# A hybrid decoder step: last down part by column halves, squares beside it, its adds and the eighth mixed row on VectorE

## The chip, the cores and the metric

The kernel runs on one core of a Trainium2 chip. The metric is the device time of one execution in microseconds (us), the median of several runs. PE is TensorE (PEld its weight loads), DVE is VectorE, ACT is ScalarE, POOL is GpSimd, SP is SyncE, which issues most DMAs.

## What is computed

One layer over a prompt of 2048 tokens and eight samples of 4 tokens (2080 columns of 1024 channels): an mLSTM branch and a windowed attention branch, merged by sigmoid gates, and then a gated feed-forward block with a causal convolution, all in float32.

```python
ga, gb = jnp.split(jax.nn.sigmoid(gt), 2, axis=-1)
mixed = ga * (h_m @ p['w_a'][l]) + gb * (h_a @ p['w_b'][l])
x = x + mixed @ p['w_out'][l]
xn = rmsnorm(x, p['g_ffn'][l])
u = xn @ w_up                                   # 1024 -> 2 * 2816
c = b_conv + sum(w_conv[tap] * ext[:, tap:tap + S] for tap in range(3))
a, g = jnp.split(c, 2, axis=-1)
h = gelu(a) * g
x = x + h @ w_down                              # 2816 -> 1024
x = rmsnorm(x, p['g_final'])                    # mean of squares over the 1024 channels of a token
```

## The kernel before

Channels lie on the partitions (KT = 8 rows of 128), tokens on the columns. Every float32 product is made of a high and a low half of each operand: the weight's high half is written by ACT (`w_high`, L2469), its low half by DVE (`w_low`, L2719), and `product` issues two matmuls of high weights (L2376) for one of low weights (L2381) in each step of the sum.

Three phases follow each other; the change is in the last, `ffn_phase`. There every engine walks one list, `PLAN`, and does at each unit what belongs to it.

- **Spans.** Five spans of 416 columns. Each has eight `branch` units (row i of the mixed gates: DVE multiplies both gates by PSUM, L2888 and L2892; POOL adds the two, L2951; ACT and DVE split the sum into halves, L2503 and L2759) and eight `out` units (w_out). The norm of a span (column sum on PE, `root` on ACT, `invert` on DVE at L2764, `x_normed` at L2770) is taken during the next span; that of span 4, the last, during the first tiles of pair 0.
- **Column pairs.** Then three pairs of column halves (348, 348 and 344 columns each). A pair has 22 tiles of seven up products (`q` units, q2.6 being product 6 of tile 2), with Strassen sums of the input made by DVE and ACT (`prep_sums` L2781 to L2786, `prep_lows` L2792 to L2797, `prep_sums_high` L2521). DVE takes the products out of PSUM (`c22` L2805, `c21` L2811), applies the convolution (`taps`) and multiplies with the gelu (`product` L2831, `g_low` L2837).
- **Down parts.** Between the tiles stand six down parts of a pair, over 4, 4, 4, 4, 4 and 2 tiles. A `down` unit is one output row: two column halves into two of the three banks ps5, ps6 and ps7, which go round. Early parts are added into the residual by DVE (L2920). In pairs 0 and 1 the last two parts (`SEEDED` and above) are seeded: ACT writes the residual into PSUM ahead (L2582) and reads the sum back (L2587). In the last pair no part is seeded. The last part's product has six matmuls for a half.
- **Final norm.** `final_square` (ACT, L2620) squares a half row into a two-buffer ring, `final_total` (POOL, L2989) adds it up, `final_sum` (PE, L2396) sums over the partitions, `final_root` (ACT, L2626), `final_invert` (DVE, L2843), and `y_normed` (DVE, L2850) multiplies. For pairs 0 and 1 this lies in the next pair's first tiles; for the last pair it stands behind the last part, where `weighted` (ACT, L2631) has multiplied by the gain and DVE by the reciprocal (L2940).
- **Weights.** SP loads each unit's split weights into a ring of six chunks, `f_wh` and `f_wl` (L2224); in pair 0 they are made from float32 weights and stored (L2215).

## Time and profile before

| | us |
|---|---|
| three runs | 2860.35, 2861.37, 2864.24 |
| median | 2861.37 |
| the profiled execution's own time | 2858.3 |
| its span in the trace | 2856.5 |

The span is what the engines' records cover; 1.8 us lie around it. The profiled execution is 3.1 us below the median. In the trace `PE` is busy for 2764.0 us. The ffn phase runs from about 1100 us to the end: the five spans to 1424 us, pair 0 to 1894 us, pair 1 to 2368 us, pair 2 to 2835 us, and then the last norm.

A row of the timeline gives a start, a busy time, the engine, the line, what is written from what, and in square brackets how long the engine had been idle and whose instruction ended that.

### The profile page before, as it was taken

Reading aid. Unit: us, or ns where it says so; the run is one execution under the profiler, and the core shown is the slowest. Engines: PE = TensorE matmul, PEld = TensorE weight load, DVE = VectorE, ACT = ScalarE, POOL = GpSimd, SP = SyncE. Lnnn points to the kernel's source line nnn. Section 1 sums busy time; section 2 is a strip of 40 time slices with the busy share of each in tenths; the row PEclk is TensorE's granted clock in tenths of the full one; section 3 lists DMA queues with packets and bytes.
Section 4 is the critical chain, followed back from the end, with each engine's and each line's share of the span. In section 5 each row is a group of like instructions: output and inputs, shape, how many; then the busy total and the mean of one; then the engine's idle time right before and its main releaser. Section 6 shows DMA issues by size and latency. Waiting matters only on the chain. (4 is left out here: it accounts for less than half of the span.)

```text
span 2856.5 us, 47085 instructions
## 1 busy us (share of the span) xinstructions
PE 2764.0 (97%) x17306; PEld 2646.6 (93%) x17306; DVE 1747.3 (61%) x2752; ACT 1323.3 (46%) x2520; POOL 431.2 (15%) x663
## 2 busy tenths in 40 slices
PE   8999999999999999999989999999999999999997
PEld 8888799989998989999989999999999998999997
DVE  5212167676767668877887777856544456445554
ACT  4212235454555445555655444773443366333442
POOL 2111021211112222222200000020000003001112
PEclk9999999999999999999999999999999999999998
DMA  5534266556655458777676666767665566755654
GB/s 186 195 128 144 89 206 189 187 161 217 215 165 162 134 201 254 258 265 259 219 281 208 211 212 221 252 204 250 203 200 172 188 204 198 244 185 188 205 194 120
DMA packets 373684, 569.44 MB, mean 199 GB/s; under 512 B 50578, under 2 KB 197586, under 8 KB 373458
## 3 DMA queue, kind: packets, MB, share of 16 engines
q1 hardware_dynamic: 371346, 566.31, 60.3%
q8 instruction: 141, 2.31, 0.3%
q14 instruction: 85, 0.70, 0.1%
q10 hardware_dynamic: 2112, 0.13, 0.0%
HBM read 415.33 MB, written 152.02 MB: 199 GB/s over the span
## 5 line engine op out<-in xcount | busy, mean ns | idle before, releaser
L2376 PE MATMUL f_ps<-f_xt,f_wh 128*128 128x348 f32 (+1 forms) x3696 | 670.6, 324 | 18.8 <-DVE both_high L2805 12.0
L2376 PEld LDWEIGHTS f_ps<-f_xt,f_wh 128*128 128x128 f32 x3696 | 604.9, 190 | 25.0 <-DVE both_high L2805 16.7
L2719 DVE TENSOR_TENSOR f_wl<-both_high,f_wh 128x512 fp32r<-128x512 f32 (+1 forms) x494 | 357.1, 736 | 203.8 <-ACT f_wh L2469 200.1
L2469 ACT ACTIVATE f_wh<-both_high 128x512 fp32r<-128x512 f32 (+1 forms) x494 | 298.8, 621 | 339.6 <-PE f_ps L2381 265.2
L2376 PE MATMUL f_ps<-f_gbuf,f_wh 128*128 128x348 f32 (+1 forms) x2112 | 383.6, 322 | 14.3 <-ACT f_ps L2582 6.3
L2381 PE MATMUL f_ps<-f_xt,f_wl 128*128 128x348 f32 (+1 forms) x1848 | 371.0, 323 | 0.0
L2376 PEld LDWEIGHTS f_ps<-f_gbuf,f_wh 128*128 128x128 f32 x2112 | 342.5, 188 | 19.9 <-ACT both_low L2587 10.0
L2381 PEld LDWEIGHTS f_ps<-f_xt,f_wl 128*128 128x128 f32 x1848 | 309.3, 189 | 0.0
L829 PE MATMUL pp<-gxh,gwh 128*128 128x416 f32 x792 | 290.9, 367 | 1.5 <-DVE gxl L778 1.3
L829 PE MATMUL pp<-gxh,gwl 128*128 128x416 f32 x792 | 279.4, 353 | 0.0
L829 PE MATMUL pp<-gxl,gwh 128*128 128x416 f32 x792 | 278.1, 351 | 0.0
L2381 PE MATMUL f_ps<-f_gbuf,f_wl 128*128 128x348 f32 (+1 forms) x1056 | 214.5, 321 | 0.0
L2920 DVE TENSOR_TENSOR both_low<-f_ps,both_low 128x348 f32<-128x348 f32 (+1 forms) x224 | 114.2, 516 | 160.3 <-PE f_ps L2381 159.6
L2381 PEld LDWEIGHTS f_ps<-f_gbuf,f_wl 128*128 128x128 f32 x1056 | 176.1, 188 | 0.0
L2946 POOL TENSOR_TENSOR f_oc<-both_high,both_low 128x2 f32<-128x2 f32 (+1 forms) x176 | 52.4, 310 | 794.5 <-DVE both_high L2805 602.7
L770 DVE TENSOR_TENSOR gwl<-both_low,gwh 128x1024 fp32r<-128x1024 f32 x100 | 122.6, 1227 | 68.5 <-ACT gwh L764 68.5
L829 PEld LDWEIGHTS pp<-gxh,gwh 128*128 128x128 f32 x792 | 149.0, 188 | 15.0 <-issue 6.9
L2820 DVE SCALAR_TENSOR_TENSOR both_high<-both_high,both_low 128x696 f32<-128x696 f32 (+2 forms) x176 | 129.4, 756 | 41.3 <-ACT both_high L2596 41.2
L829 PEld LDWEIGHTS pp<-gxl,gwh 128*128 128x128 f32 x792 | 149.8, 189 | 1.6
L829 PEld LDWEIGHTS pp<-gxh,gwl 128*128 128x128 f32 x792 | 149.0, 188 | 1.6
L2596 ACT ACTIVATE both_high<-both_high,both_low 128x696 f32<-128x696 f32 (+2 forms) x176 | 137.7, 814 | 1.0 <-DVE both_high L2811 1.0
L2824 DVE SCALAR_TENSOR_TENSOR both_high<-both_high,both_low 128x696 f32<-128x696 f32 (+2 forms) x176 | 129.9, 759 | 4.7
(342 smaller groups left out, 4441.8 us busy)
## 6 DMA issues: line engine op xcount, KB each, us to landing
both_high<-in_w_up SPq DMA_DIRECT2D x220, 256.0 KB, 4.2
f_wh<-up_parts SPq DMA_DIRECT2D x176, 256.0 KB, 2.7
f_wl<-up_parts SPq DMA_DIRECT2D x176, 256.0 KB, 3.0
both_low<-in_w_gate SPq DMA_DIRECT2D x80, 512.0 KB, 4.6
up_parts<-f_wh SPq DMA_DIRECT2D x88, 256.0 KB, 2.9
up_parts<-f_wl SPq DMA_DIRECT2D x88, 256.0 KB, 3.4
both_high<-in_w_br SPq DMA_DIRECT2D x40, 512.0 KB, 4.7
both_high<-in_w_out SPq DMA_DIRECT2D x40, 512.0 KB, 4.5
```

Source lines behind the costliest of these rows:

```text
L770: dve.tensor_tensor(wl[u % GWS][:], raw[u % GRAWS], wh[u % GWS][:].bitcast(F32), ALU.subtract).then_inc(ev("gw_lo"), 1)
L829: mm = pe.matmul(pp[:, u % 2, 0:TB], w[u % GWS][:, j * P:j * P + P], x[:, j, :], start=(j == 0 and w is wh and x is xh), stop=(j == KT - 1 ...
L2376: pe.matmul(out, cut(wh, k), x(k), start=(start and k == 0 and x is xhi), stop=False, skip_group_check=not start or not stop)
L2381: mm = pe.matmul(out, cut(wl, k), xhi(k), start=False, stop=(stop and k == K - 1), skip_group_check=not start or not stop)
L2469: act.activation(ring_slot(wh, e, w), src, ACT.Copy).then_inc(ev("w_hi"), 1)
L2596: ins = act.activation(o, t, ACT.Identity, bias=taps[:, f, 4 * s + 3:4 * s + 4], scale=taps[:, f, 4 * s + 2:4 * s + 3])
L2719: dve.tensor_tensor(ring_slot(wl, e, w), src, ring_slot(wh, e, w).bitcast(F32), ALU.subtract).then_inc(ev("w_lo"), 1)
L2820: ins = dve.scalar_tensor_tensor(o, t, tap(1), o, ALU.mult, ALU.add)
L2824: ins = dve.scalar_tensor_tensor(o, t, tap(0), o, ALU.mult, ALU.add)
L2920: dve.tensor_tensor(t, ps[BANK[v][s]][:, 0:w], t, ALU.add).then_inc(ev(f"ps_read{BANK[v][s]}"), 1)
L2946: return pool.tensor_tensor(dst, src, unit.to_broadcast(list(src.shape)), ALU.mult)
```

## The change

- **Last part of the last pair.** It becomes sixteen `half` units, the eight rows of column half 0 and then those of half 1, each with one bank and its own load of the weight chunk (sixteen loads of two times 128 KB instead of eight). The norm goes by halves too: `final_sum` of half 0 after half unit 11, its root on ACT after unit 12, its reciprocal on DVE behind the add of unit 13, the first four rows of `y_last` behind the adds of units 14 and 15. `weighted` is gone (the gain is in `y_last`), and y is stored in four transfers for each half.
- **Pairs 0 and 1.** The sixteen squares (ACT) and totals (POOL) of the final norm stand beside the last part's own units instead of in the next pair's first eight units; sum, root, reciprocal (in two halves) and `y_normed` come about a tile earlier. The norm of span 4 moves from tiles 0 and 1 to tiles 1 and 2 of pair 0.
- **Last part of pairs 0 and 1.** Its adds are DVE's, two in each unit; only part 4 (`i // KT == SEEDED`) is seeded.
- **Spans.** The eighth mixed row's add is DVE's instead of POOL's.

```diff
-            units += [("down", p, KT * part + o) for o in range(KT)]
+            if p == END and part + 1 == len(PARTS):
+                units += [("half", p, KT * s + o) for s in range(2) for o in range(KT)]
+            else:
+                units += [("down", p, KT * part + o) for o in range(KT)]
...
-    return kind == "down" and p < END and i // KT >= SEEDED or kind == "out" and p == SPANS - 1
+    return kind == "down" and p < END and i // KT == SEEDED or kind == "out" and p == SPANS - 1
...
-    fsq, facc = [nrm[:, WIDE * i:WIDE * i + WIDE] for i in range(2)], nrm[:, 2 * WIDE:4 * WIDE]
+    fsq, facc = [slot["s3"][:, 0:WIDE], slot["s4"][:, 0:WIDE]], high[:, AHEAD_G:AHEAD_G + 2 * WIDE]
...
-    span4_at = {AT["q", 0, 5]: (0, 1), AT["q", 0, 6]: (2, 3), AT["q", 1, 1]: (4, 5), AT["q", 1, 3]: (6, 7)}
+    span4_at = {AT["q", 1, 5]: (0, 1), AT["q", 2, 0]: (2, 3), AT["q", 2, 2]: (4, 5), AT["q", 2, 4]: (6, 7)}
...
+    final_place = lambda p, x: (x % KT, x // KT) if p == END else (x // 2, x % 2)
+    for _p in range(PAIRS):
+        for x in range(2 * KT):
+            k, _s = final_place(_p, x)
+            _v = AT["half", END, x] if _p == END else AT["down", _p, KT * (len(PARTS) - 1) + k] + 1
+            fin_sq.setdefault(_v, []).append((_p, x))
...
-        for x in range(2 * KT):
-            fin_sq.setdefault(AT["q", _n + x // 2 // NQ, x // 2 % NQ], []).append((_p - 1, x))
-        for k, (g, j) in enumerate(((2, 2), (2, 4), (2, 5), (3, 0), (3, 1), (3, 3), (3, 4), (3, 6))):
+        for k, (g, j) in enumerate(((1, 2), (1, 4), (1, 5), (2, 0), (2, 1), (2, 3), (2, 4), (2, 6))):
             fin_y[AT["q", _n + g, j]] = (_p - 1, k)
-    fin_sum = {AT["q", FT * p + 1, 6]: p - 1 for p in range(1, PAIRS)}
+    fin_sum = {AT["q", FT * p, 4]: p - 1 for p in range(1, PAIRS)}
...
-    fin_invert = {AT["q", FT * p + 2, 1]: p - 1 for p in range(1, PAIRS)}
+    fin_invert = {AT["q", FT * p + s, 6 if s == 0 else 1]: (p - 1, s) for p in range(1, PAIRS) for s in range(2)}
...
-    xres_at = {AT["q", FT * p + 3 + j, 2]: (p, j) for p in range(1, PAIRS) for j in range(2)}
+    xres_at = {AT["q", FT * p + 3, 4 * j]: (p, j) for p in range(1, PAIRS) for j in range(2)}
...
-            if v == AT["q", 0, 3]:
+            if v == AT["q", 1, 3]:
                 root(SPANS - 1)
...
+                if i == KT - 1:
+                    for x in range(2):
+                        evacuated(dve, v, x)
+                    dve.tensor_tensor(gate_tile(i, 0), gate_tile(i, 0), gate_tile(i, 1), ALU.add).then_inc(ev("mixed_last"), 1)
...
+            if v == AT["half", END, KT + 5]:
+                final_invert(END, 0)
+            for k in {KT + 6: (0, 1), KT + 7: (2, 3)}.get(i if kind == "half" else 0, ()):
+                y_last(0, k)
...
-        final_invert(END)
...
+        for k in range(4, KT):
+            y_last(0, k)
+        final_invert(END, 1)
         for k in range(KT):
-            dve.wait_ge(ev("y_weighted"), k + 1)
-            t = two(xres[:, k, 0:2 * w])
-            dve.tensor_tensor(t, t, two(facc)[:, :, 0:w], ALU.mult).then_inc(ev("y_ready"), 1)
+            y_last(1, k)
```

The squares' and totals' buffers move from `f_nrm` to buffers that part 5 leaves free (`both_high`); the line numbers of the changed kernel are 27 to 37 higher on DVE. Three places of DVE's queue follow. In the order's names `f_wl<-both_high,f_wh` is `w_low`.

At the end of tile 0 of pair 0, before: the reciprocal (`f_rinv`) and the norm of span 4 (`x_normed`) stand between the evacuations `c22` and `c21`.

```order
L2805 TENSOR_TENSOR both_high<-both_high,f_ps3 128x348
L2719 TENSOR_TENSOR f_wl<-both_high,f_wh 128x512
L2764 RECIPROCAL f_rinv<-f_rinv 128x416
L2770 SCALAR_TENSOR_TENSOR both_low<-both_low,f_gffn,f_rinv 128x416 x2
L2811 TENSOR_TENSOR both_high<-f_ps4,both_high 128x348
L2719 TENSOR_TENSOR f_wl<-both_high,f_wh 128x512
L2770 SCALAR_TENSOR_TENSOR both_low<-both_low,f_gffn,f_rinv 128x416 x2
L2742 TENSOR_TENSOR both_high<-both_high 128x512
L2719 TENSOR_TENSOR f_wl<-both_high,f_wh 128x512
```

The same queue after, now at the end of tile 1:

```order
L2746 TENSOR_TENSOR f_wl<-both_high,f_wh 128x512 x2
L2858 TENSOR_TENSOR both_high<-both_high 128x696
L2832 TENSOR_TENSOR both_high<-both_high,f_ps3 128x348
L2746 TENSOR_TENSOR f_wl<-both_high,f_wh 128x512
L2791 RECIPROCAL f_rinv<-f_rinv 128x416
L2797 SCALAR_TENSOR_TENSOR both_low<-both_low,f_gffn,f_rinv 128x416 x2
L2838 TENSOR_TENSOR both_high<-f_ps4,both_high 128x348
L2746 TENSOR_TENSOR f_wl<-both_high,f_wh 128x512
```

The reciprocal and the first `x_normed` now stand behind `c22` of tile 1 instead of that of tile 0, each with the weights' low halves around them.

In the last part of pair 0 DVE before makes the next pair's sums and lows (`f_xt`) and low halves of weights:

```order
L2719 TENSOR_TENSOR f_wl<-both_high,f_wh 128x256
L2792 TENSOR_TENSOR f_xt<-both_high,f_xt 128x348
L2794 TENSOR_TENSOR f_xt<-both_high,f_xt 128x696
L2797 TENSOR_TENSOR f_xt<-both_high,f_xt 128x1392
L2719 TENSOR_TENSOR f_wl<-both_high,f_wh 128x256
L2781 TENSOR_TENSOR both_high<-f_nrm 128x348
L2782 TENSOR_TENSOR both_high<-f_nrm 128x348
L2784 TENSOR_TENSOR both_high<-both_high,f_nrm 128x348
L2786 TENSOR_TENSOR both_high<-f_nrm,both_high 128x348
L2719 TENSOR_TENSOR f_wl<-both_high,f_wh 128x256
```

And after:

```order
L2811 TENSOR_TENSOR both_high<-both_high 128x348
L2813 TENSOR_TENSOR both_high<-both_high 128x348
L2746 TENSOR_TENSOR f_wl<-both_high,f_wh 128x256
L2957 TENSOR_TENSOR both_low<-f_ps7,both_low 128x348
L2957 TENSOR_TENSOR both_low<-f_ps5,both_low 128x348
L2819 TENSOR_TENSOR f_xt<-both_high,f_xt 128x348
L2821 TENSOR_TENSOR f_xt<-both_high,f_xt 128x696
L2824 TENSOR_TENSOR f_xt<-both_high,f_xt 128x1392
L2746 TENSOR_TENSOR f_wl<-both_high,f_wh 128x256
L2957 TENSOR_TENSOR both_low<-f_ps6,both_low 128x348
L2957 TENSOR_TENSOR both_low<-f_ps7,both_low 128x348
L2808 TENSOR_TENSOR both_high<-f_nrm 128x348
```

The adds `both_low<-f_ps,both_low` now stand between the sums and the lows, so each pair of adds is queued behind four or three preparation steps; before, ACT did this work.

At the end of the program DVE before adds the last halves, takes one reciprocal and multiplies eight whole rows:

```order
L2920 TENSOR_TENSOR both_low<-f_ps5,both_low 128x344
L2920 TENSOR_TENSOR both_low<-f_ps6,both_low 128x344
L2920 TENSOR_TENSOR both_low<-f_ps7,both_low 128x344
L2843 RECIPROCAL f_nrm<-f_nrm 128x2x344
L2940 TENSOR_TENSOR both_low<-both_low,f_nrm 128x688 x8
```

And after:

```order
L2971 TENSOR_TENSOR both_low<-f_ps7,both_low 128x344
L2971 TENSOR_TENSOR both_low<-f_ps5,both_low 128x344
L2870 RECIPROCAL both_high<-both_high 128x344
L2971 TENSOR_TENSOR both_low<-f_ps6,both_low 128x344
L2883 SCALAR_TENSOR_TENSOR both_low<-both_low,f_gfin,both_high 128x344 x2
L2971 TENSOR_TENSOR both_low<-f_ps7,both_low 128x344
L2883 SCALAR_TENSOR_TENSOR both_low<-both_low,f_gfin,both_high 128x344 x6
L2870 RECIPROCAL both_high<-both_high 128x344
L2883 SCALAR_TENSOR_TENSOR both_low<-both_low,f_gfin,both_high 128x344 x8
```

The first half's reciprocal, and two of its rows, stand ahead of the last add; the second half has a reciprocal and eight half rows behind it.

## Rows read from the trace of the kernel before

**Rows 1.** The page's busy times: us, share of the span, instructions.

```profile
PE 2764.0 (97%) x17306; PEld 2646.6 (93%) x17306; DVE 1747.3 (61%) x2752; ACT 1323.3 (46%) x2520; POOL 431.2 (15%) x663
```

**Rows 2.** Timeline of PE: units before which it was idle longest, in brackets.

```profile
1141.62 0.45 PE L2376 MATMUL f_ps<-f_mh,f_wh 128*128 128x416 f32 x1 [1.48 <-DVE f_ml L2759]
...
1434.98 2.69 PE L2376 MATMUL f_ps<-f_xt,f_wh 128*128 128x348 f32 x8 [5.51 <-DVE both_high L2805]
...
1482.20 1.51 PE L2376 MATMUL f_ps<-f_gbuf,f_wh 128*128 128x348 f32 x8 [1.88 <-issue]
...
1876.99 0.89 PE L2376 MATMUL f_ps<-f_gbuf,f_wh 128*128 128x348 f32 x4 [0.70 <-ACT f_ps L2582]
...
1887.25 0.87 PE L2376 MATMUL f_ps<-f_gbuf,f_wh 128*128 128x348 f32 x4 [1.50 <-ACT f_ps L2582]
...
1936.87 1.54 PE L2376 MATMUL f_ps<-f_xt,f_wh 128*128 128x348 f32 x8 [2.81 <-DVE both_high L2805]
...
2360.95 0.87 PE L2376 MATMUL f_ps<-f_gbuf,f_wh 128*128 128x348 f32 x4 [1.48 <-ACT f_ps L2582]
...
2411.11 2.66 PE L2376 MATMUL f_ps<-f_xt,f_wh 128*128 128x344 f32 x8 [3.65 <-DVE both_high L2805]
...
2434.32 1.50 PE L2376 MATMUL f_ps<-f_xt,f_wh 128*128 128x344 f32 x8 [0.61 <-DMA f_wh<-up_parts]
```

**Rows 3.** Windows: stretch, us, busy PE, PEld, DVE, ACT, POOL, PEclk, DMA share, GB/s.

```profile
1434.00:1442.00 8.00, 7.02 (x28) 7.02 (x29) 5.88 (x10) 3.61 (x8) 0.78 (x2) 0.59 0.94 309
...
2411.00:2417.00 6.00, 5.88 (x21) 5.89 (x22) 3.42 (x6) 2.04 (x5) 1.82 (x4) 0.52 0.94 288
```

**Rows 4.** Timeline of DVE and POOL at the eighth mixed row of span 0.

```profile
1138.74 2.16 DVE L2719 TENSOR_TENSOR f_wl<-both_high,f_wh 128x512 fp32r<-128x512 f32 x2
...
1138.96 1.39 POOL L2951 TENSOR_TENSOR f_gates<-f_gates 128x416 f32<-128x416 f32 x1 [2.19 <-DVE f_gates L2892]
```

**Rows 5.** Windows, the first 30 us of pair 0; then the timeline of DVE.

```profile
1424.00:1454.00 30.00, 24.49 (x138) 24.20 (x137) 26.68 (x40) 17.47 (x31) 3.50 (x8) 0.89 0.66 219
```

```profile
1431.35 1.21 DVE L2770 SCALAR_TENSOR_TENSOR both_low<-both_low,f_gffn,f_rinv 128x416 f32<-128x416 f32 x2
...
1450.20 0.51 DVE L2805 TENSOR_TENSOR both_high<-both_high,f_ps 128x348 f32<-128x348 f32 x1
```

**Rows 6.** Windows in pair 0's last part; ACT's seed; DVE's add in pair 2.

```profile
1873.00:1888.00 15.00, 10.63 (x62) 9.44 (x61) 11.86 (x20) 13.90 (x30) 0.62 (x2) 1.00 0.69 227
```

```profile
1887.47 0.47 ACT L2582 ACTIVATE f_ps<-both_low 128x348 f32<-128x348 f32 x1
```

```profile
2820.72 0.52 DVE L2920 TENSOR_TENSOR both_low<-f_ps,both_low 128x344 f32<-128x344 f32 x1 [0.43 <-PE f_ps L2381]
```

**Rows 7.** Timeline at the start of pair 1: POOL's totals, then DVE.

```profile
1899.83 9.58 POOL L2989 TENSOR_TENSOR f_nrm<-f_nrm 128x348 f32<-128x348 f32 x10 [0.41 <-ACT f_nrm L2620]
```

```profile
1904.87 1.05 DVE L2719 TENSOR_TENSOR f_wl<-both_high,f_wh 128x512 fp32r<-128x512 f32 x1 [0.20 <-ACT f_wh L2469]
...
1928.67 4.49 DVE L2843 RECIPROCAL f_nrm<-f_nrm 128x696 f32<-128x696 f32 x1
```

**Rows 8.** Timeline of the tail: POOL, then PE, ACT and DVE.

```profile
2825.81 11.28 POOL L2989 TENSOR_TENSOR f_nrm<-f_nrm 128x344 f32<-128x344 f32 x12 [0.20 <-ACT f_nrm L2620]
```

```profile
2837.15 1.42 PE L2396 MATMUL f_ps<-f_nrm,both_low 128*128 128x344 f32 x4 [2.23 <-POOL f_nrm L2989]
...
2837.53 1.28 ACT L2626 ACT_TABLE_LOAD   x1
2838.82 0.99 ACT L2626 ACTIVATE f_nrm<-f_ps,f_eps 128x344 f32<-128x344 f32 x2
2839.84 4.45 DVE L2843 RECIPROCAL f_nrm<-f_nrm 128x688 f32<-128x688 f32 x1 [4.37 <-ACT f_nrm L2626]
2844.33 6.37 DVE L2940 TENSOR_TENSOR both_low<-both_low,f_nrm 128x688 f32<-128x688 f32 x8
```

**Rows 9.** Windows: parts 4 and 5 of pair 2, columns as in the other windows.

```profile
2806.00:2822.00 16.00, 16.00 (x104) 16.00 (x103) 4.98 (x10) 0.49 (x1) 0.15 (x1) 1.00 0.26 75
```

More of the change, by code:

```diff
@@ L1854, in banks @@
             mine = [5 + (d + s) % BANKS_D for s in range(2)]
+        elif kind == "half":
+            mine = [5 + (2 * len(DOWN_AT) + i) % BANKS_D]
         bank.append(mine)
@@ L1858, in banks @@
             count[m] += 1
-        if kind != "down":
+        if kind not in ("down", "half"):
             closed = list(count)
@@ L1869, in whole_product @@
     kind, n, i = PLAN[v]
-    return kind == "down" or kind == "q" and PRODUCTS[i][0][0] == "s"
+    return kind in ("down", "half") or kind == "q" and PRODUCTS[i][0][0] == "s"
 def pair_at(v):
     kind, n, _ = PLAN[v]
-    return n if kind == "down" else n // FT
+    return n if kind in ("down", "half") else n // FT
 STORED = [whole_product(v) and pair_at(v) == 0 for v, _ in CHUNK]
@@ L1892, in chunk_of_pair @@
     kind, n, i = PLAN[v]
-    return FIRST[AT["down", 0, i]] if kind == "down" else QC[n % FT][i]
+    if kind == "half":
+        i = KT * (len(PARTS) - 1) + i % KT
+    return QC[n % FT][i] if kind == "q" else FIRST[AT["down", 0, i]]
 def split_until(v):
@@ L2102, in part_rows @@
         kind, n, i = PLAN[v]
-        return (downs[i], PARTS[i // KT] * P) if kind == "down" else (ups[tile_of(n), int(PRODUCTS[i][0][1]) - 1], QUAD)
+        if kind == "half":
+            i = KT * (len(PARTS) - 1) + i % KT
+        return (downs[i], PARTS[i // KT] * P) if kind != "q" else (ups[tile_of(n), int(PRODUCTS[i][0][1]) - 1], QUAD)
     def slot_stored(engine, e):
@@ L2420, in _ @@
                                 start=not seeded(v))
+            elif kind == "half":
+                n, s, w = BANK[v][0], i // KT, WIDTH[b]
+                wait(pe, f"ps_read{n}", BEFORE[v][0])
+                g0 = FT * b + BEGIN[-2]
+                wait(pe, "g_lo", FT * PAIRS)
+                cut = lambda x, k: gh[(g0 + k) % SLOTS_G][x][:, w * s:w * s + w]
+                product(ps[n][:, 0:w], FIRST[v], PARTS[-1], lambda k: cut(0, k), lambda k: cut(1, k))
             elif kind == "out":
@@ L2455, in _ @@
             if v in fin_sum:
-                final_sum(fin_sum[v])
-        final_sum(END)
+                for s in range(2):
+                    final_sum(fin_sum[v], s)
+            if v == AT["half", END, KT + 3]:
+                final_sum(END, 0)
+        final_sum(END, 1)
     @block.scalar
@@ L2501, in mixed_high @@
         def mixed_high(b, o):
-            wait(act, "mixed", KT * b + o + 1)
+            if o < KT - 1:
+                wait(act, "mixed", (KT - 1) * b + o + 1)
+            else:
+                wait(act, "mixed_last", b + 1)
             act.activation(mh[:, o, :], gate_tile(o, 0), ACT.Copy).then_inc(ev("mixed_hi"), 1)
@@ L2697, in _ @@
             if v in fin_root:
-                final_root(fin_root[v])
-            if kind == "down" and b == END and i // KT + 1 == len(PARTS):
-                for x in (2 * (i % KT), 2 * (i % KT) + 1):
-                    final_square(END, x)
-                if i % KT:
-                    weighted(i % KT - 1)
-        weighted(KT - 1)
-        final_root(END)
+                for s in range(2):
+                    final_root(fin_root[v], s)
+            if v == AT["half", END, KT + 4]:
+                final_root(END, 0)
+        final_root(END, 1)
         for k in range(0, KT, MO):
-            act.wait_ge(ev("y_ready"), KT * END + k + MO)
+            act.wait_ge(ev("y_ready"), KT * (END + 1) + k + MO)
             for h, lo, hi, x in pair_halves(END)[1:]:
@@ L2982, in final_total @@
         def final_total(p, x):
-            k, s = x // 2, x % 2
+            k, s = final_place(p, x)
             w = WIDTH[p]
@@ L2995, in _ @@
         for v, (kind, b, i) in enumerate(PLAN):
-            if kind == "branch":
+            if kind == "branch" and i < KT - 1:
                 mix(b, i)
@@ L3011, in _ @@
                 final_total(p, x)
-            if kind == "down" and b == END and i // KT + 1 == len(PARTS):
-                for x in (2 * (i % KT), 2 * (i % KT) + 1):
-                    final_total(END, x)
 def build(nc, a):
```

87 lines of the change are left out of this document (50 added, 37 removed).

## Prediction

> **What bounds the kernel now.** I read the page's busy times first: PE is busy for 97% of the span and no other engine for more than 61% [rows 1]. So PE sets the time, and a change can pay in three ways only: it closes a gap of PE, it spares a stretch in which PE runs at the low clock, or it shortens the tail in which PE is done. The work on PE itself stays the same. Next the timeline of PE with its idle times [rows 2]: in the ffn phase it shows nearly all the gaps, and each names who ended it. Five places matter here: the eighth row of a span (1.48 us behind DVE's low half, five spans, about 7 in all); `c22` in tile 1 of pair 0 (5.51); four slots of the last part of pair 0 and four of pair 1, all behind ACT (0.70 to 1.50 each; they add up to 4.4 and 3.4, and with smaller ones the stretches are 5.7 and 4.9 longer than sixteen matmul slots need); `c22` at the start of pairs 1 and 2 (2.81 and 3.65); and waits for weights of 1.88 and 0.61. Third, the windows: after the gaps at 1434 and 2411 the granted clock is 0.59 and 0.52 [rows 3], the low level of 1.2 GHz for part of the stretch; the eight matmuls there take 2.69 and 2.66 instead of about 1.5 [rows 2], which costs 2.7 us a time with those behind them. After 1936.87 the eight took 1.54: a gap of 2.81 brought no drop. Last the tail: from 2837.15 on there is one chain [rows 8], ending 5.8 us after DVE's last multiply at 2850.7, in the last stores' landing.
>
> **The eighth mixed row.** Before: gate multiply, POOL's add 1.39, ACT's half 0.55, DVE's half 0.59 [rows 4]. DVE's add is one more 416-column TENSOR_TENSOR, the same form as the 0.59 one, so the chain is 0.8 us shorter. But DVE's queue also has two `w_low` that took 2.16 beside POOL's add [rows 4]; without POOL I take 1.3, and they are what is late next: the low half can start about 0.4 earlier. So 0.38 for each of five spans, **+1.9**. Ends: 0, and 7.4 if the whole gap closed, which DVE's queue excludes as far as I can follow it.
>
> **Start of pair 0.** Taking root, reciprocal and `x_normed` of span 4 out of tile 0 relieves q1.6: walking ACT's and DVE's queues, the 5.51 gap becomes about 3.1. But the same work now lies in tiles 1 and 2, where DVE is nearly full: 26.68 busy of 30 us [rows 5]. The reciprocal (2.7 us: 416 columns at the 4.49 for 696 of [rows 7]) and a pair of `x_normed` at 1.21 [rows 5] come just behind `c22` of tile 1, and three more pairs lie in the next tile. `c22` of tile 2, at 1450.20 before [rows 5], comes at about 1453.1, after a gap of some 6 us and with a drop of the clock behind it like the one at 1434. PE reaches the third tile's end 4.5 us later than before; 1.5 of that disappears in the gap of 1.88 at 1482.20, where the transfers are what is late. **-3.0**. Ends: -6 (none disappears, and the first drop stays too) and +3 (the first gap closes and DVE keeps up; +8 with no drop at all).
>
> **Last parts of pairs 0 and 1.** ACT's two copies per half (0.47 here [rows 6], the reading one alike) were the limit, since ACT also had the high halves: 13.90 busy of 15 us while PE was busy 10.63 [rows 6]. They are replaced with one DVE add of 0.52 a half [rows 6]. But DVE was itself busy 11.86 of these 15 us [rows 6] with the next pair's sums, lows and low weights; the six adds that fall in the stretch bring 3.1 more, 15.0 in 15. And the order matters: each pair of adds stands behind three or four of those, and the ring has only three banks, so PE runs out of banks after three halves. I get gaps of 2.0, 1.25 and 2.35 instead of the four, and the next pair starting at 1894.2 instead of 1894.4: +0.2 for pair 0, +0.45 for pair 1. POOL's totals are now beside it. The trace shows that beside them [rows 7] a `w_low` took 1.05 instead of 0.69, and I count -0.7 and -0.45 for that: **-0.5** and **0**. Ends: +5.7 and +4.9 if DVE kept up; -2 each from the collisions.
>
> The Trainium skill's page on SBUF (SBUF — State Buffer, "SBUF: two separate sides") says that VectorE with two SBUF inputs and GpSimd reading SBUF hold a shared port pair in turn, each for a whole instruction, the other fully blocked. The row agrees in kind; by that rule every total of about 0.95 could block a preparation step in full, which is rival B.
>
> **Start of pairs 1 and 2.** The sixteen squares and totals leave the next pair's first units, and the reciprocal of 696 columns, 4.49 in one piece [rows 7], which stood ahead of `c22`, becomes two of 2.25, the first a tile earlier. By the queues pair 1 has one gap of 0.9 instead of 2.81, with 0.5 gained from `w_low` no longer beside totals: **+2.4**. Pair 2 has gaps of 1.4 and 0.7 instead of 3.65, and, all of them being below the 2.81 that kept the clock, no drop: 1.55 + 2.75 = **+4.3**. Ends: 0 and 0 if `c22` waits for the ACT that now stands earlier; +3 and +6.4. The waits for weights behind the loads of the residual (0.61 [rows 2], two others alike) have more room: **+0.8**, ends 0 and 1.7.
>
> **The tail.** What went on after the last matmul at 2834.9: POOL's last total until 2837.1, sum 1.42 for both halves, table 1.28, root 0.99, reciprocal 4.45, eight multiplies of 0.80 [rows 8]. Now half 0 goes through sum, table and root beside the last matmuls; its sum costs PE 0.45. Its reciprocal (2.25) starts at 2835.45 and the adds of units 14 and 15 wait behind it, the last ending about 2840.2. Square 0.5, total 0.95, sum 0.7 and root 0.6 of half 1 bring 2842.7; DVE has meanwhile done half 0's rows; reciprocal until 2844.95; eight half-row multiplies of 0.49 (half of 0.94 for 696) until 2848.9, against 2850.7: +1.8. The last store is half as large: +0.9. **+2.7** (ends 0 and +4). What this adds: the adds of units 14 and 15 behind the reciprocal, for which the last square waits 3.3 us.
>
> **The loads of the last part.** Sixteen chunks of 256 KB instead of eight, one each 0.945 us: 277 GB/s. Before, 75 GB/s took a share of 0.26 [rows 9], so full use would be 288. Six chunks of the ring give a lead of 4.7 us, against a landing of some 3. I take 0. The stores of the convolution rows, issued behind these loads, come 5 us later and are over by the time y leaves.
>
> **Sum.** 1.9 - 3.0 - 0.5 + 0 + 2.4 + 4.3 + 0.8 + 2.7 = +8.6. The profiled execution of 2858.3 would be 2849.7; with the 3.1 by which the median lies above it, **2852.8**.
>
> **Rivals.** *A. DVE keeps up in the last parts.* For it: its own idle time there (3.1 of 15) equals the adds. Against: it is needed at other moments. It gives 10.6 - 0.6 of the other limits' slack, so 2843. *B. The totals hold up DVE.* Sixteen totals now run beside the sums, lows and low weights. If a step waits for half a total (0.47), the sixteen steps that meet one cost 7.5 a pair, of which half falls into DVE's waits: -3.7 twice, 2860. For: the 1.05. Against: the adds read PSUM, and [rows 8] shows POOL busy in one piece at 0.94 a total while DVE's add takes 0.52 [rows 6] there too. *C. The halved tail brings nothing* because the first reciprocal holds the last adds for as long as it saves: 2855.5. The change doesn't do what it says in that case. *D. Slower: the last part's loads.* It decides when a chunk takes longer than the 0.945 of its unit. At 2 us a chunk (131 GB/s) the last part is 16 x 1.05 - 4.7 = 12.1 longer, and a drop of the clock adds 2.7: 2868. For it: 277 of 288 GB/s is no reserve, and each load's packets are half as long as an ordinary chunk's. Against: loads of this size landed without a gap of PE in [rows 9]'s stretch.
>
> **How the numbers follow.** Forecast 0.48 (own range 2848 to 2857, from the ends of the start of pair 0 and of pairs 1 and 2), A 0.15, B 0.20, C 0.08, D 0.09. The range reaches from 2844 to 2862: it leaves out D and half of A. A measurement of this kernel can tell about 0.2%, 5.7 us, from no change, so faster is below 2855.7 and slower above 2867.1. Faster: 0.39 of the forecast, A, a little of B and half of C, 0.60. Slower: D and a bad corner of B, 0.10. The same: 0.30.
>
> **What would show it.** Right: at each span's eighth row a gap of 1.1; in tile 1 of pair 0 a gap of 3 without and in tile 2 one of 6 with a low clock; in the last parts three gaps that end with DVE's add instead of ACT's seed; no low clock at 2411; DVE's last multiply 1.8 earlier. Wrong: gaps of PE in the last part of pair 2 released by a DMA (D), steps with two SBUF inputs near 1 us throughout the last parts (B), no gap there at all (A). The weakest step is the start of pair 0, where a queue walked decides over a low clock or none.

## The result

| | us |
|---|---|
| before, median of 17 runs | 2861.37 (2857.22 to 2864.40) |
| changed kernel, median of 17 runs | 2867.89 (2862.93 to 2871.49) |
| ratio | 1.0024, 95% interval 1.0018 to 1.0031 |
| the profiled execution's span, before and changed | 2856.5 and 2865.8 |

The changed kernel is slower by 0.24%, where 0.3% faster was forecast. Rows of PE's timeline in the trace of the changed kernel follow, each with the wait ahead of it in brackets; they answer to [rows 2], which has no row for the second. L2392 is the line of the high weights' matmuls, L2416 the column sum.

```profile
1140.27 0.46 PE L2392 MATMUL f_ps<-f_mh,f_wh 128*128 128x416 f32 x1 [1.14 <-DVE f_ml L2786]
...
1399.33 2.69 PE L2392 MATMUL f_ps<-f_xt,f_wh 128*128 128x348 f32 x8 [4.15 <-DVE f_xt L2824]
...
1430.82 1.61 PE L2392 MATMUL f_ps<-f_xt,f_wh 128*128 128x348 f32 x8 [3.10 <-DVE both_high L2832]
...
1451.29 2.69 PE L2392 MATMUL f_ps<-f_xt,f_wh 128*128 128x348 f32 x8 [5.23 <-DVE both_high L2832]
...
1485.30 1.51 PE L2392 MATMUL f_ps<-f_gbuf,f_wh 128*128 128x348 f32 x8 [2.48 <-issue]
...
1885.11 0.92 PE L2392 MATMUL f_ps<-f_gbuf,f_wh 128*128 128x348 f32 x4 [1.75 <-DVE both_low L2957]
...
1895.98 1.53 PE L2392 MATMUL f_ps<-f_gbuf,f_wh 128*128 128x348 f32 x4 [5.02 <-DVE both_low L2957]
...
1931.78 1.55 PE L2392 MATMUL f_ps<-f_xt,f_wh 128*128 128x348 f32 x8 [1.01 <-DVE both_high L2832]
...
2372.55 1.53 PE L2392 MATMUL f_ps<-f_gbuf,f_wh 128*128 128x348 f32 x4 [5.99 <-DVE both_low L2957]
...
2408.67 1.53 PE L2392 MATMUL f_ps<-f_xt,f_wh 128*128 128x344 f32 x8 [1.16 <-DVE both_high L2832]
...
2438.34 1.99 PE L2392 MATMUL f_ps<-f_xt,f_wh 128*128 128x344 f32 x8 [2.24 <-DMA f_wh<-up_parts]
...
2852.97 1.52 PE L2416 MATMUL f_ps<-both_high,both_low 128*128 128x344 f32 x2 [5.98 <-POOL both_high L3033]
```

The eighth mixed row's gap is 1.14 instead of 1.48, as forecast, but not in every span: the kernel before has it in four spans (1 to 4; in span 0 PE does not wait, and [rows 4] show span 1), and in the last of these it is still 1.48. The gap of 4.15 at the start of pair 0 is as it was (4.13 at 1401.24 before), with a low clock behind it in both. In pair 0 the one gap of 5.51 is now two, 3.10 and 5.23. In the last parts ACT's seed no longer ends the gaps; small ones remain (1.75 in pair 0, 0.88 and 0.53 in pair 1), and one of 5.02 and one of 5.99 are new. At the start of the next pairs 1.01 and 1.16 stand where 2.81 and 3.65 stood. A wait for weights has grown from 0.61 to 2.24. And the column sum waits 5.98 for POOL, with half 0 of the norm already done.

The granted clock in windows (columns as in [rows 3]) shows what lies behind those gaps:

```profile
1430.00:1438.00 8.00, 7.18 (x35) 7.18 (x36) 7.96 (x11) 3.86 (x7) 1.19 (x2) 0.79 0.46 165
1448.00:1456.00 8.00, 4.71 (x16) 4.71 (x17) 6.16 (x11) 3.42 (x7) 0.77 (x2) 0.58 0.89 269
1484.00:1490.00 6.00, 4.71 (x21) 4.74 (x22) 4.20 (x6) 1.52 (x3) 0.35 (x1) 0.73 1.00 337
1885.00:1890.00 5.00, 4.89 (x20) 4.44 (x21) 4.97 (x12) 1.37 (x1) 0.00 (x0) 0.66 0.43 153
1896.00:1904.00 8.00, 8.00 (x39) 8.00 (x40) 4.24 (x9) 3.87 (x8) 6.73 (x9) 0.76 0.36 105
```

PE runs at the low level of 1.2 GHz for part of the time behind 1430.82, 1451.29, 1485.30, 1885.11 and 1895.98 (the five windows), and behind 2372.55 (1.53 for four matmuls) and 2438.34 (1.99 for eight). Before, these places had one such stretch at 1434 and one at 2411 [rows 3]; the latter is gone, since eight matmuls take 1.53 at 2408.67. From the start to the last sum, the low stretches of the clock record add up to 37.5 us in the trace of the kernel before and 58.0 in that of the changed one.

**Where the time went.** Up to the last part of the last pair PE does the same matmuls in the same order in all these kernels (the column sums of the final norm stand some hundred matmuls earlier where the squares are moved), so the start of the same matmul (counted from the first) can be compared. The table gives how much each profiled execution lost (+) or gained (-) against that of the kernel before, in us. Its stretches are named by that kernel's times: up to 1390 (both first phases and the spans); 1390 to 1830 (pair 0 up to its last part, with span 4's norm); 1830 to 1945 (last part of pair 0 and start of pair 1); 1945 to 2320; 2320 to 2450 (last part of pair 1 and start of pair 2); and from 2790 on (the tail). The last two columns are the span's difference and the median of its runs.

| kernel | to 1390 | to 1830 | to 1945 | to 2320 | to 2450 | tail | span | median |
|---|---|---|---|---|---|---|---|---|
| changed | -1.9 | +6.9 | +3.4 | -0.4 | +3.2 | -2.0 | +9.3 | 2867.89 |
| e1_head_late | +2.7 | +7.6 | +0.0 | -0.7 | -1.8 | -2.4 | +5.5 | 2864.54 |
| e2_span4_back | +2.6 | +0.9 | +3.1 | -0.6 | +0.5 | -2.3 | +4.1 | 2859.84 |
| e3_seeds_back | +5.0 | +6.9 | +6.6 | -0.9 | +3.3 | -2.4 | +18.6 | 2872.80 |
| e4_head_span4 | -0.4 | -1.3 | +1.6 | -0.8 | -1.7 | -2.3 | -4.9 | 2853.85 |
| e5_tail_only | +5.1 | +0.4 | -1.5 | +0.3 | -1.9 | -2.3 | +0.2 | 2855.73 |
| e6_adds_no_squares | +0.5 | +0.3 | -1.7 | +0.6 | -4.0 | -2.4 | -6.8 | 2854.95 |
| e7_squares_late | +0.7 | -0.4 | -1.7 | -0.6 | -1.0 | -2.4 | -5.5 | 2854.49 |
| e8_late_seeds | +4.7 | -0.0 | +0.7 | +1.1 | +0.8 | -2.3 | +4.9 | 2859.10 |
| e9_inv_late | +3.4 | +0.5 | -1.5 | +0.9 | -1.5 | -3.2 | -1.5 | 2853.09 |
| e10_no_row | +1.4 | -0.7 | -1.6 | +1.2 | -0.7 | -2.9 | -3.2 | 2852.09 |
| e11_xres_old | +4.6 | +4.0 | -0.2 | +0.6 | -1.6 | -3.2 | +4.3 | 2854.81 |
| e12_span4_split | +0.1 | -1.1 | -1.7 | +0.5 | -3.7 | -3.2 | -9.0 | 2854.68 |

The first column warns: all but e5, e10 and e12 are the changed kernel up to 1390, and yet it runs from -1.9 to +5.0. Executions with the same instructions can lie 7 us apart there, so one trace's span says little; the later columns, each tied to gaps that one can see, say more, though chance is in them too (+4.0 up to 1830 in e11). The changed kernel's own sum is plain: +6.9 at the start of pair 0, +3.4 and +3.2 round the last parts, -2.0 in the tail. In the stretch round pair 0's last part PE is idle hardly longer than before, 8.3 us against 7.8, but busy 110.1 us against 107.2 with the same matmuls: the low clock behind the two new gaps is most of what was lost there.

**What holds the last parts.** POOL's timeline in the last part of pair 0, then ACT's, then DVE's:

```profile
1891.40 0.35 POOL L2990 TENSOR_TENSOR both_high<-f_oc,both_low 128x2 f32<-128x2 f32 x2 [43.38 <-DVE f_xt L2824]
1891.70 1.49 POOL L2990 TENSOR_TENSOR both_high<-both_high,both_low 128x348 f32<-128x348 f32 x2
1893.15 7.58 POOL L3033 TENSOR_TENSOR both_high<-both_high 128x348 f32<-128x348 f32 x8
```

```profile
1892.57 0.49 ACT L2656 ACTIVATE both_high<-both_low 128x348 f32<-128x348 f32 x1 [3.84 <-POOL both_high L2990]
...
1893.69 0.61 ACT L2499 ACTIVATE f_wh<-both_high 128x512 fp32r<-128x512 f32 x1
```

```profile
1889.66 1.60 DVE L2824 TENSOR_TENSOR f_xt<-both_high,f_xt 128x1392 fp32r<-128x1392 f32 x1
1894.33 1.16 DVE L2746 TENSOR_TENSOR f_wl<-both_high,f_wh 128x512 fp32r<-128x512 f32 x1 [3.08 <-ACT f_wh L2499]
1895.42 1.36 DVE L2957 TENSOR_TENSOR both_low<-f_ps,both_low 128x348 f32<-128x348 f32 x3
...
1901.58 0.69 DVE L2746 TENSOR_TENSOR f_wl<-both_high,f_wh 128x512 fp32r<-128x512 f32 x1 [0.20 <-ACT f_wh L2499]
```

POOL had been idle for 43.38 us and was released at 1891.40 by DVE's last step of the next pair's preparation (`f_xt`, L2824). What it then did first is `head`, two copies that open the next pair's first tile (L2990, 128x2; at pair 1 there are four). They wait for the whole preparation, because the tile's buffers are used by it. Behind them in POOL's queue stand the first totals (L2990, 128x348, then L3033), whose squares are ready since 1884.6. The squares have a ring of two buffers, so ACT's third square waits for the first total: 3.84 idle, until 1892.57. Behind it in ACT's queue is the high half of a weight (1893.69), DVE's low half waits for that (1894.33, after 3.08 idle), and behind it stand DVE's adds (1895.42), for which PE's three banks wait. So POOL stood for DVE's preparation, ACT for POOL, DVE for ACT, PE for DVE. The same chain stands in pair 1.

### The profile page after: what moved, and what is told of

Read it like the earlier page. It is cut to its first block, busy times and chain, and to the rows that moved or that the text cites. A ratio compares the mean times of both kernels' runs of the same rounds, so it can differ in the third digit from the quotient of the medians.

```text
span 2865.8 us, 47025 instructions
## 1 busy us (share of the span) xinstructions
PE 2770.4 (97%) x17306; PEld 2653.7 (93%) x17306; DVE 1762.9 (62%) x2800; ACT 1293.8 (45%) x2448; POOL 423.7 (15%) x658
## 4 chain that ended last, share of the span: by engine, by line
PE 51%; DVE 8%; issue 2%; ACT 1%; DMA 1%; SPq 1%; POOL 1%; DVEq 0%; ACTq 0%; POOLq 0%
PE f_ps L2392 34%; PE f_ps L2397 17%; DVE f_wl L2746 2%; DMA f_wh<-up_parts 1%; DVE both_low L2797 1%; DVE f_rinv L2791 0%; DVE f_xspan L2797 0%; DVE f_xt L2824 0%; DVE both_high L2847 0%; DVE f_ml L2786 0%; POOL both_high L3033 0%; DVE f_gates L2921 0%; DMA both_high<-in_w_dn 0%; DVE f_gates L2925 0%; SPq L2328 0%
## 5 line engine op out<-in xcount | busy, mean ns | idle before, releaser
L2392 PE MATMUL f_ps<-f_xt,f_wh 128*128 128x348 f32 (+1 forms) x3696 | 670.2, 324 | 18.7 <-DVE both_high L2832 11.0
L2392 PEld LDWEIGHTS f_ps<-f_xt,f_wh 128*128 128x128 f32 x3696 | 604.8, 190 | 24.6 <-DVE both_high L2832 15.9
L2392 PE MATMUL f_ps<-f_gbuf,f_wh 128*128 128x348 f32 (+1 forms) x2112 | 389.1, 325 | 21.5 <-DVE both_low L2957 14.2
L2392 PEld LDWEIGHTS f_ps<-f_gbuf,f_wh 128*128 128x128 f32 x2112 | 347.5, 190 | 26.8 <-DVE both_low L2957 17.5
L2957 DVE TENSOR_TENSOR both_low<-f_ps,both_low 128x348 f32<-128x348 f32 (+1 forms) x240 | 121.6, 516 | 163.7 <-PE f_ps L2397 162.9
L2990 POOL TENSOR_TENSOR f_oc<-both_high,both_low 128x2 f32<-128x2 f32 (+1 forms) x176 | 52.2, 308 | 821.6 <-DVE both_high L2832 617.4
```

What stands on the lines that cost most here:

```text
L2392: pe.matmul(out, cut(wh, k), x(k), start=(start and k == 0 and x is xhi), stop=False, skip_group_check=not start or not stop)
L2957: dve.tensor_tensor(t, ps[BANK[v][s]][:, 0:w], t, ALU.add).then_inc(ev(f"ps_read{BANK[v][s]}"), 1)
L2990: return pool.tensor_tensor(dst, src, unit.to_broadcast(list(src.shape)), ALU.mult)
```

## The experiments

Two things were to be told apart in the last parts: a queue (theory Q, the chain above) or a full VectorE (rival V); and apart from that, what the move of span 4's norm costs.

**e1_head_late.** The opening copies stand behind the totals.

```diff
+            if kind == "q" and b > 0 and b % FT == 0 and i == 0:
+                for s in (0, 1):
+                    head(b, s)
...
-                    if n + 1 < FT * PAIRS:
+                    if n + 1 < FT * PAIRS and (n + 1) % FT:
                         for s in (0, 1):
                             head(n + 1, s)
```

> The changed kernel, with one edit: POOL's two copies that open the next pair's first tile (`head`) stand behind the last part's totals instead of ahead of them. Theory Q (a queue on POOL): those copies wait for the last of the next pair's lows, the totals stand behind them, the ring of two squares fills, ACT holds at its third square with the high half of a weight behind it, and DVE's low half and adds follow. Then the gaps of 5.02 and 5.99 in the last parts go, with the low clock behind them: about 5 us less in each, 10 in all, 2858. Rival V (VectorE is full): the adds are late because DVE has the preparation ahead of them; then the copies don't matter and at most 2 us are saved.

Measured: 2864.54 (2859.13 to 2867.38), ratio to before 1.0009 (1.0 to 1.0018): 3.35 less than the changed kernel by the medians, a third of what Q gave. In its trace the gaps of 5.02 and 5.99 are 3.07 and 3.45. So Q is about half of it: the wait is real and goes with its cause, but something else holds the adds next. By the table the two stretches round the last parts lost 8.4 us less; the medians give 3.35, and with span 4's norm at its old place (e4 against e2) 6.0.

**e2_span4_back.** The norm of span 4 at its old places.

```diff
-    span4_at = {AT["q", 1, 5]: (0, 1), AT["q", 2, 0]: (2, 3), AT["q", 2, 2]: (4, 5), AT["q", 2, 4]: (6, 7)}
+    span4_at = {AT["q", 0, 5]: (0, 1), AT["q", 0, 6]: (2, 3), AT["q", 1, 1]: (4, 5), AT["q", 1, 3]: (6, 7)}
...
-            if v == AT["q", 1, 3]:
+            if v == AT["q", 0, 3]:
                 root(SPANS - 1)
```

> The changed kernel with the norm of span 4 (root, reciprocal, x_normed, its stores) back at its old places in tiles 0 and 1 of pair 0. Theory: that move alone cost the 6.6 us by which PE falls behind between the end of the spans and tile 4; so 6.5 less, 2861.5. Rival: other parts of the change (the mixed row's shift, the transfers of the down weights) cost part of it, and 3 or less come back, 2865.

Measured: 2859.84 (2857.90 to 2862.89), ratio 0.9996 (0.9987 to 1.0005): 8.0 less than the changed kernel. By the medians it is the dearest part of the change. The stretch to 1830 lost 6.9, 7.6 and 6.9 in the three kernels with the norm moved, and between -1.3 and +0.9 in e2 and e4 to e10 with it at its old place. e11 has it there too and lost 4.0, with neither of the two gaps: its waits at the down parts of pair 0 are longer, and it has a low stretch at 1664. PE in e2, the same units as 1430.82 and 2372.55 above:

```profile
1437.86 2.69 PE L2392 MATMUL f_ps<-f_xt,f_wh 128*128 128x348 f32 x8 [5.52 <-DVE both_high L2832]
...
2370.50 1.53 PE L2392 MATMUL f_ps<-f_gbuf,f_wh 128*128 128x348 f32 x4 [5.98 <-DVE both_low L2957]
```

The gap of 5.52 is back and no second one follows, and the new gap of the last part of pair 1 is untouched, 5.98.

**e3_seeds_back.** The last part is seeded by ACT as before (`i // KT >= SEEDED`), with squares beside it.

> The changed kernel with the last part of pairs 0 and 1 seeded by ACT again (no adds on DVE), squares still beside it. Theory Q: ACT now has the squares, which wait for POOL, ahead of the seeds, so the gap stays or grows: no gain, 2868 to 2872. Rival V: with the adds off DVE the gaps of 5 to 6 us go and the four of 1 us return: 2861 to 2863.

Measured: 2872.80 (2868.83 to 2876.95), ratio 1.0040 (1.0027 to 1.0052), slower than the changed kernel by 4.9. V alone does not explain the gap: without an add on DVE it is still there, and ACT's seed ends it, since the seeds stand behind the same square:

```profile
1904.06 1.50 PE L2392 MATMUL f_ps<-f_gbuf,f_wh 128*128 128x348 f32 x4 [5.66 <-ACT f_ps L2615]
```

**e4_head_span4.** Both edits.

> Both edits in one kernel: the opening copies behind the totals, and span 4's norm at its old places. If both theories hold and the parts are apart, 10 + 6.5 less than the changed kernel: 2851, below the kernel before by 10. If V holds, 2860.

Measured: 2853.85 (2850.98 to 2858.06), ratio 0.9977 (0.9966 to 0.9987). Faster than both kernels, 7.4 below the kernel before measured beside it (2861.27). The forecast of 2851 was 2.9 too good, again because a gap of 3 us stays. Its trace shows the rest of the cause. DVE, POOL and PE in the last part of pair 0:

```profile
1883.52 2.35 DVE L2824 TENSOR_TENSOR f_xt<-both_high,f_xt 128x1392 fp32r<-128x1392 f32 x1
1885.79 1.40 DVE L2746 TENSOR_TENSOR f_wl<-both_high,f_wh 128x512 fp32r<-128x512 f32 x1
1887.12 1.36 DVE L2957 TENSOR_TENSOR both_low<-f_ps,both_low 128x348 f32<-128x348 f32 x3
```

```profile
1883.05 9.38 POOL L3033 TENSOR_TENSOR both_high<-both_high 128x348 f32<-128x348 f32 x8 [3.94 <-ACT both_high L2656]
```

```profile
1887.68 0.92 PE L2392 MATMUL f_ps<-f_gbuf,f_wh 128*128 128x348 f32 x4 [3.09 <-DVE both_low L2957]
```

While POOL's totals run in one piece from 1883.05 on, DVE's 1392-column step takes 2.35, against 1.60 in the changed kernel at 1889.66, where no total ran beside it, and the low half of a weight takes 1.40, against 0.69 there at 1901.58, between two groups of totals; [rows 7] has one of 1.05 beside totals. The adds, which read PSUM, stand behind both and keep their length. This agrees with the rule of the Trainium skill that the prediction cites (SBUF — State Buffer, "SBUF: two separate sides"), in that steps with two SBUF inputs are held and the adds are not: three of those took 1.36 together, here and in the changed kernel.

**e5_tail_only.** The kernel before with the half units and the tail alone (its reciprocals at pairs 1 and 2 are two halves in a row, at q2.0 and q2.1).

> The kernel before with the change's last part of the last pair alone: half units, their loads, the norm by halves; squares of pairs 0 and 1, seeds, mixed row and span 4's norm as before. My theory: the tail gives what it gave in the changed kernel, where the end of the span lies 1.7 us less behind than PE at the start of the part: 1.5 to 2.7 less than before, 2859 to 2860. Rival C: it brings nothing, 2861.

Measured: 2855.73 (2853.01 to 2861.06), ratio 0.9988 (0.9979 to 0.9997), 4.6 below the kernel before measured beside it (2860.32), more than expected. Its tail is 2.3 shorter. The table shows where the rest is: -1.5 and -1.9 at the starts of pairs 1 and 2. In these the only difference is the reciprocal of 696 columns in two pieces, the first a unit earlier and with other steps between them: the gaps there are 1.33 and 2.12 instead of 2.81 and 3.65.

**e6_adds_no_squares.** Adds on DVE, tail and row of the changed kernel; squares in the next pair, norm of span 4 at its old places.

```diff
-            _v = AT["half", END, x] if _p == END else AT["down", _p, KT * (len(PARTS) - 1) + k] + 1
+            _v = AT["half", END, x] if _p == END else AT["q", FT * (_p + 1) + x // 2 // NQ, x // 2 % NQ]
```

> The changed kernel without the moved squares (they stand in the next pair's first units again, with all that follows them) and with span 4's norm at its old places; the last part's adds are still DVE's. If POOL's totals made the gaps, both by the queue and by lengthening DVE's steps, the last parts now have gaps of about 1.7, 0.9 and 1.5 at most, DVE's steps there keep 1.60 and 0.69, and PE loses nothing against before in these parts: 2861.4 - 1.5 for the mixed row - 1.7 for the tail = 2858. If DVE is full by itself (V), gaps of 3 us and more stay and it is 2863.

Measured: 2854.95 (2851.56 to 2860.07), ratio 0.9981 (0.9973 to 0.9990). The gaps in the last parts are 1.76 and 1.54, and 1.22, 0.50 and 2.01, all behind DVE's adds: close to the 2.0, 1.25 and 2.35 of the prediction's walk. In pair 0:

```profile
1880.73 1.01 PE L2392 MATMUL f_ps<-f_gbuf,f_wh 128*128 128x348 f32 x4 [1.76 <-DVE both_low L2957]
...
1887.96 0.91 PE L2392 MATMUL f_ps<-f_gbuf,f_wh 128*128 128x348 f32 x4 [1.54 <-DVE both_low L2957]
```

From the start of the last part to the start of the next pair PE gains 0.2 and 0.3 us on the kernel before, where the walk, before its allowance for the totals, had 0.2 and 0.45. So the adds are sound by themselves, and worth next to nothing: 0.8 less than e5, within the spread, though the row's add is in that too. The whole loss in the last parts came with the squares, and V is out.

**e7_squares_late.** Squares and totals three units later, behind the preparation.

```diff
-            _v = AT["half", END, x] if _p == END else AT["down", _p, KT * (len(PARTS) - 1) + k] + 1
+            _v = AT["half", END, x] if _p == END else AT["down", _p, KT * (len(PARTS) - 1) + k] + 4
```

> The changed kernel with span 4's norm at its old places and the squares and totals of pairs 0 and 1 three units later (row k at unit k + 4 of the last part, the last ones in the next pair's first units), so that they come behind the preparation; sum, root and reciprocals two or three units later. If the overlap of totals and preparation is what is left of the gaps after the queue on POOL is mended, this beats the kernel with both edits (2853.9): no gap over 2.5 in the last parts, no low clock there, 2850. If not, it is the same as that one.

Measured: 2854.49 (2851.90 to 2859.91), ratio 0.9981 (0.9972 to 0.9990). The gaps are as expected (1.77, 0.41 and 1.20 in pair 0, 2.01 the longest in pair 1). By its trace the last parts gain 0.2 and lose 1.2 against before, where e4 loses 3.4 and 3.3, so the overlap of totals and preparation costs something. But the median is that of e4. Part of what is saved is late elsewhere: the starts of the pairs gain a little less than in e4, and in pair 2 two gaps follow. By the table 2.4 us should be left between 1830 and 2450, and the medians do not show them. PE in pair 2, and the SP queue before these gaps:

```profile
2424.33 1.49 PE L2392 MATMUL f_ps<-f_xt,f_wh 128*128 128x344 f32 x8 [1.60 <-DMA f_wh<-up_parts]
...
2434.90 1.51 PE L2392 MATMUL f_ps<-f_xt,f_wh 128*128 128x344 f32 x8 [0.72 <-DMA f_wh<-up_parts]
```

```profile
2422.71 0.51 SPq L2238 DMA_DIRECT2D f_wl<-up_parts  x1
2427.55 0.37 SPq L2301 DMA_DIRECT2D both_low<-x_rows  x1
```

SP issued nothing from 2423.2 to 2427.55; the load of the residual (L2301) waits there until y's stores have landed, with the parts' loads behind it.

**e8_late_seeds.** As e7, seeded by ACT.

> As the last one, and the last part seeded by ACT again. The last parts would have the four gaps of the kernel before (4.4 and 3.4 us); whether DVE's adds or ACT's seeds are better is the difference of the two: by the walk in the prediction 0.2 and 0.45 us for the adds, so the same within 1 us, 2850 to 2851.

Measured: 2859.10 (2853.62 to 2865.83), ratio 0.9996 (0.9987 to 1.0005): 4.6 above e7, where the same was expected. With late squares ACT has sixteen squares and sixteen seeds in the second half of the part: besides the old gaps there is one of 1.02 in pair 0 and another of 1.02 in pair 1, both behind ACT's seed, and the two stretches lose 2.4 and 1.8 more than in e7. So the adds on DVE are worth something once ACT has the squares too; without them, e6 against e5, they are not seen to be.

**e9_inv_late.** As e7; in the tail the reciprocal of half 0 behind all adds.

```diff
-            if v == AT["half", END, KT + 5]:
-                final_invert(END, 0)
...
+        final_invert(END, 0)
+        for k in range(KT):
+            y_last(0, k)
```

> The kernel with late squares and span 4's norm at its old places (2854.5), and in the last pair the reciprocal of half 0 behind the last add instead of between the adds of units 13 and 14. In the changed kernel the adds of units 14 and 15 waited for that reciprocal (2.3 us) and two multiplies, and the last square, total and sum behind them. My theory of the tail: without this the root of half 1 is done 3.5 us earlier, and VectorE's own work after the last add (two reciprocals of 2.3 and sixteen multiplies of 0.49) then sets the end: 1.5 less, 2853. Rival: the stores or VectorE's multiplies are the limit anyhow, 2854.5.

Measured: 2853.09 (2849.12 to 2857.48), ratio 0.9977 (0.9968 to 0.9986), 1.4 less than e7, which the spread does not settle; the tails in the traces do: -3.2, -2.9, -3.2 and -3.2 in the four kernels with this edit, -2.3 to -2.4 in the eight others but the changed one. DVE in the changed kernel's tail and in e9's:

```profile
2847.16 2.30 DVE L2870 RECIPROCAL both_high<-both_high 128x344 f32<-128x344 f32 x1 [1.49 <-ACT both_high L2661]
...
2849.50 0.52 DVE L2971 TENSOR_TENSOR both_low<-f_ps,both_low 128x344 f32<-128x344 f32 x1
...
2855.17 2.29 DVE L2870 RECIPROCAL both_high<-both_high 128x344 f32<-128x344 f32 x1
...
2857.49 3.99 DVE L2883 SCALAR_TENSOR_TENSOR both_low<-both_low,f_gfin,both_high 128x344 f32<-128x344 f32 x8
```

```profile
2837.57 2.29 DVE L2870 RECIPROCAL both_high<-both_high 128x344 f32<-128x344 f32 x1
2839.90 4.59 DVE L2883 SCALAR_TENSOR_TENSOR both_low<-both_low,f_gfin,both_high 128x344 f32<-128x344 f32 x8
2844.41 2.29 DVE L2870 RECIPROCAL both_high<-both_high 128x344 f32<-128x344 f32 x1
2846.73 3.99 DVE L2883 SCALAR_TENSOR_TENSOR both_low<-both_low,f_gfin,both_high 128x344 f32<-128x344 f32 x8
```

In the changed kernel the add of unit 14 comes 2.3 us after the reciprocal began, and the second reciprocal waits until 2855.17. In e9 the sum's wait is 3.66 instead of 5.98 and DVE works without a pause.

**e10_no_row.** As e9, with the eighth mixed row's add on POOL.

> As the last one, with the eighth mixed row's add back on POOL. The changed kernel's gaps there were 1.14 in four spans and 1.48 in one, against 1.48 in all five: so undoing it costs 4 x 0.34 = 1.4 more than the last one.

Measured: 2852.09 (2850.24 to 2857.57), ratio 0.9975 (0.9966 to 0.9983). Not slower than e9. The expectation counted a gap too many: there are four, and three of them are 1.48 again instead of 1.14 (the fourth is 1.48 or a little more in every kernel). So the row is worth 1.0 us in a trace, not 1.4, and it drowns: the stretch to 1390 was +1.4 here and +3.4 in e9. This is the fastest median measured, 8.7 below the kernel before measured beside it (2860.76); e4, e6, e7, e9, e11 and e12 cannot be told from it.

**e11_xres_old.** As e9, `xres_in` at q3.2 and q4.2.

> As the kernel with the reciprocal behind the adds, with the load of the residual (xres_in) at its old two places, q3.2 and q4.2 instead of q3.0 and q3.4. In the run with late squares SP stood 4.3 us before that load, which waits for the stores of y to land, and the parts behind it came late: gaps of 1.60 and 0.72 at the third and fourth tile of pair 2, released by a DMA. With the load further back the gaps should be 0.6 or none: 1 to 2 us less, 2851.5. Rival: the stores themselves fill the queue, and nothing changes.

Measured: 2854.81 (2849.53 to 2862.60), ratio 0.9979 (0.9970 to 0.9987). The time is the rival's: a gap of 2.18 behind the same kind of load instead of 1.51, and no gain. That SP's wait makes the parts late is thus not shown; the stores and loads of that stretch may just be too many. It stays open.

**e12_span4_split.** As e10, with four of span 4's rows behind `c22` of tile 1.

> The last kernel but one (POOL's add of the eighth row, late squares, reciprocal behind the adds; 2852.1) with half of the moved work moved: of span 4's norm the root, the reciprocal and the first four rows stay in tile 0 of pair 0, the other four rows (two pairs of x_normed, 2.3 us of VectorE) go behind c22 of tile 1, to q1.5 and q2.0. Theory: VectorE is full from tile 0 to tile 2, so what is taken out of the first gap (5.51 to about 3.2) comes back as a second gap of some 2.5 us in tile 2, and what counts is whether the clock falls twice. With one low stretch: the same within 1 us. With two, as in the changed kernel: 2 to 4 more, 2855. Rival: there is slack in tile 1, the second gap stays out, and it is 2 us faster, 2850.

Measured: 2854.68 (2849.28 to 2857.26), ratio 0.9974 (0.9963 to 0.9986), the same as e10. PE's gaps:

```profile
1433.06 2.69 PE L2392 MATMUL f_ps<-f_xt,f_wh 128*128 128x348 f32 x8 [4.39 <-DVE both_high L2829]
...
1449.33 1.55 PE L2392 MATMUL f_ps<-f_xt,f_wh 128*128 128x348 f32 x8 [1.23 <-DVE both_high L2829]
```

5.51 became 4.39 and 1.23, sum 5.62, with one low stretch: what leaves the first gap comes back in the second. Moving less does no harm, and brings nothing.

## The prediction, point by point

The range of 2844 to 2862 did not hold 2867.89, and the sign was wrong. The terms summed to +8.6; between the two traces it is -9.3. By its own steps, each measured by the start of the same matmul in the two traces (+ is gained):

- **The eighth mixed row**, +1.9 forecast for five spans. The size foreseen (0.38) is right, 0.34, but only in three spans: the prediction took five gaps of 1.48, about 7 us in all, where the trace had four, and one of them did not move. So it is 1.0, below what runs can show (e9 and e10). Why the last one stayed was not looked into.
- **Start of pair 0**, -3.0 forecast, -6.9 in the trace, 8.0 by e2. The gaps came as walked: 3.10 (about 3.1) and 5.23 (some 6), the second with the low clock. At the third tile's end PE is 4.4 us later than before, against 4.5 in the prediction (3.2 and 3.9 in e1 and e3). There is luck in this: the clock fell behind 3.10 too, which the sum left out, and the second gap was shorter. The term that failed is the next one, the 1.5 us that were to vanish in the gap of 1.88. Instead that gap grew, to 2.48 (1485.30; 2.38 and 2.48 in e1 and e3), and had a low stretch of its own behind it, here and in e1: 2.1 us more. What PE waited for there the profile does not say (`issue`), so why it grew stays open. In all the gaps add up to 10.8 against 7.4 before (5.51 and 1.88), 3.4 more; the rest of the 6.9 is the low clock. Even the bound of -6 was passed.
- **Last parts**, -0.5 and 0 forecast, -5.2 and -5.6 in the trace, and the real failure: it alone turns the sign. The walk of DVE's queue with its adds was good, as e6 shows. But POOL's queue was not walked at all: it was said that the totals are "beside it", and nothing was asked about what stands ahead of them on POOL. `head` for the next pair stands there in both kernels; before, the totals came after the preparation, and the copies cost nothing. That this wait costs time is shown by taking it away (e1, and e4 against e2: 3.35 and 6.0 us). The second cause, the overlap, is the one of rival B, which priced it at 3.7 a pair against the 0.7 and 0.45 in the sum. e4 shows its rows (2.35 for 1.60, 1.40 for 0.69) and still loses 3.4 and 3.3 in the last parts, near B's price; with squares out of the way these are gone (e6: 0.2 and 0.3 gained). But e7, where the overlap is gone, is by its median no faster than e4, so its price is shown by traces alone.
- **Starts of pairs 1 and 2**, +2.4 and +4.3 forecast. The gaps are 1.01 (0.9) and 1.16 with 0.50 (1.4 and 0.7), without a low clock at 2408: right. From the pair's first matmul on, 1.8 is won back in pair 1, and 4.7 in pair 2 up to the waits for weights. For these +0.8 was forecast, and the changed kernel's trace has -2.3 instead, the gap of 2.24 with a low stretch. That is this execution's: in e1 to e4, with the same loads at the same places, the gap is 1.05 to 1.41 without one, and 0.1 to 0.5 is gained. And e5 shows that much of the gain at the starts needs no moved squares: cutting the reciprocal in two gives 1.5 of the 1.8 and 2.6 of the 4.7.
- **The tail**, +2.7 forecast, +2.0 in the trace, +2.3 in e5. Right. The last sum came 5.98 us after the last product; e9 to e12 show that the first reciprocal's place between the adds costs 0.8 of the tail.
- **The loads of the last part**, 0 forecast (rival D 2868). PE waited 0.15 us once for a DMA there. D gave the right time by luck, for the wrong reason.
